# Paired 512-column products and GpSimd weight sums in the fast feed-forward tiles of a two-layer transformer kernel

## The reference, cut to what matters

```
def swiglu(h, w1, w3, w2):
    return (jax.nn.silu(h @ w1) * (h @ w3)) @ w2
...
x = x + 0.5 * rms_norm(swiglu(rms_norm(x, g[0]), ffn_w1[l, 0], ffn_w3[l, 0], ffn_w2[l, 0]), g[1])
...
x = x + 0.5 * rms_norm(swiglu(rms_norm(x, g[4]), ffn_w1[l, 1], ffn_w3[l, 1], ffn_w2[l, 1]), g[5])
```

## Time and profile before

| what | value |
|---|---|
| runs | 1863.45, 1861.57, 1861.51 us; median 1861.57 us |
| profiled execution | 1861.66 us, its span 1859.7 us |
| granted TensorE clock over the span | 1.000 |
| busy | TensorE 99%, weight loads 91%, VectorE 71%, ScalarE 49%, GpSimd 3% |
| chain of waits that ended last | TensorE 85%, VectorE 9%, ScalarE 3% |
| DMA | 174.64 MB, mean 94 GB/s |

### The profile page before, as it was taken

The page is one execution under the profiler, slowest core; times in us unless marked ns, Lnnn a source line. Parts: engine busy times, 40 slices in busy tenths (PEclk is TensorE's granted clock), DMA queues, the critical chain, the costliest instruction groups (busy, mean ns, idle before and its releaser), DMA issues.

```text
span 1859.7 us, 31170 instructions
## 1 busy us (share of the span) xinstructions
PE 1842.6 (99%) x12175; PEld 1693.9 (91%) x12175; DVE 1318.0 (71%) x1742; ACT 914.3 (49%) x1386; POOL 53.6 (3%) x51
## 2 busy tenths in 40 slices
PE   8999999999999999999999999999999999999999
PEld 7899988988889899998898999989988898999888
DVE  6888862487656888882288888822888488888623
ACT  6455552355545545562255555622666464455522
POOL 0000000011100000000000000000000000000000
PEclk9999999999999999999999999999999999999999
DMA  6244343232223333333323343333221232343331
GB/s 183 80 113 113 91 115 102 79 90 72 77 57 102 91 91 106 97 104 106 108 57 108 91 113 104 102 98 104 63 63 57 69 91 84 99 112 105 109 102 47
DMA packets 339464, 174.64 MB, mean 94 GB/s; under 512 B 11070, under 2 KB 337836, under 8 KB 339372
## 3 DMA queue, kind: packets, MB, share of 16 engines
q1 hardware_dynamic: 338656, 172.25, 33.0%
q10 hardware_dynamic: 716, 1.11, 0.2%
HBM read 171.24 MB, written 2.10 MB: 93 GB/s over the span
## 4 chain that ended last, share of the span: by engine, by line
PE 85%; DVE 9%; ACT 3%; issue 2%; DMA 0%; POOL 0%; DVEq 0%; SPq 0%; ACTq 0%
PE acc L1881 19%; PE acc L1882 19%; PE acc L1883 19%; PE duo L1881 9%; PE duo L1883 9%; PE duo L1882 9%; DVE wl L1175 2%; DVE xg L1220 1%; DVE mx L1534 1%; PE acc L2147 1%; DVE probT L1555 1%; ACT prob L889 1%; DVE y L1240 1%; ACT wh L641 0%; DVE xT L1247 0%
## 5 line engine op out<-in xcount | busy, mean ns | idle before, releaser
L1881 PE MATMUL acc<-xg,wh 128*128 128x256 f32 (+1 forms) x1040 | 340.4, 327 | 2.4 <-DVE xg L1220 1.0
L1883 PE MATMUL acc<-xg,wl 128*128 128x256 f32 (+1 forms) x1040 | 336.9, 324 | 0.0
L1882 PE MATMUL acc<-xg,wh 128*128 128x256 f32 (+1 forms) x1040 | 336.8, 324 | 0.0
L1175 DVE TENSOR_TENSOR wl<-raw,wh 128x1024 fp32r<-128x1024 f32 (+2 forms) x198 | 228.9, 1168 | 126.5 <-ACT wh L641 126.2
L1882 PE MATMUL acc<-hT,wh 128*128 128x512 f32 (+1 forms) x704 | 255.2, 363 | 0.0
L1881 PE MATMUL acc<-hT,wh 128*128 128x512 f32 (+1 forms) x704 | 255.2, 363 | 0.0
L1883 PE MATMUL acc<-hT,wl 128*128 128x512 f32 (+1 forms) x704 | 255.2, 362 | 0.0
L641 ACT ACTIVATE wh<-raw 128x1024 fp32r<-128x1024 f32 (+2 forms) x198 | 194.4, 1011 | 116.4 <-PE acc L1883 71.8
L1881 PEld LDWEIGHTS acc<-xg,wh 128*128 128x128 f32 x1040 | 197.7, 190 | 20.5 <-issue 3.1
L1883 PEld LDWEIGHTS acc<-xg,wl 128*128 128x128 f32 x1040 | 197.7, 190 | 15.8
L1882 PEld LDWEIGHTS acc<-xg,wh 128*128 128x128 f32 x1040 | 197.9, 190 | 14.9
(11 more groups left out here) (283 smaller groups left out, 4175.6 us busy)
## 6 DMA issues: line engine op xcount, KB each, us to landing
raw<-in_ffn_w_dram SPq DMA_DIRECT2D x238, 512.0 KB, 4.2
raw<-in_ffn_w_dram SPq DMA_DIRECT2D x32, 384.0 KB, 3.4
raw<-in_moba_w_qkv_dram SPq DMA_DIRECT2D x24, 512.0 KB, 3.8
raw<-in_moba_w_o_dram SPq DMA_DIRECT2D x8, 512.0 KB, 3.8
raw<-in_mla_w_o_dram SPq DMA_DIRECT2D x8, 512.0 KB, 3.7
xin<-in_x_dram SPq DMA_DIRECT2D x4, 512.0 KB, 5.4
raw<-in_mla_w_dq_dram SPq DMA_DIRECT2D x4, 512.0 KB, 3.9
raw<-in_mla_w_uq_dram SPq DMA_DIRECT2D x8, 256.0 KB, 2.9
```

Source lines behind the costliest of these rows:

```text
L1175: v.tensor_tensor(wl[:, slot, 0:tiles], raw[:, slot, 0:tiles], f32(wh[:, slot, 0:tiles]), ALU.subtract).then_inc(w_lo, 1)
L1881: t.matmul(dst, w_h, m_h, start=start, stop=False, skip_group_check=onto)
L1882: t.matmul(dst, w_h, m_l, start=False, stop=False, skip_group_check=onto)
L1883: return t.matmul(dst, w_l, m_h, start=False, stop=stop, skip_group_check=onto)
```

## The change

In the fast tiles:

- `paired` takes the place of `tiles`: for each step of k one matmul with the high weights streams the high and the low part of the moving operand as 512 columns into a pair of 256-column accumulators (one bank), and one with the low weights streams the high part alone, 256 columns, onto the first of the pair. Before, there were three matmuls of 256 columns.
- Every accumulator is now a pair, so P3 gets a bank of its own (`acc[2 + j]`), `usum` is joined by `gsum` (which lies over `cosT` and `sinT`), ScalarE's copies are 512 columns each and one more, and VectorE's `gate_row` and `up_row` each add 128 x 1024 and then `fold` the pairs (128 x 512).
- The weight sums leave VectorE: GpSimd's `weight_sums` makes them with three operations per tile (128 x 512, 128 x 512, 128 x 1024). The second waits until the previous tile's third low part has read `ssum`; SyncE's `read` waits for the third as well.
- The rope tables are loaded in three of the four feed-forward stages, ahead of the down products, in place of the two earlier places.

```diff
-        usum = at("usum", [P, 4, HALF], F32, rb_at)
+        usum = at("usum", [P, 2, 2, HALF], F32, rb_at)
+        gsum = at("gsum", [P, 2, 2, HALF], F32, cos_at)
...
-            return acc[j], duo[j][:].rearrange("p (a s) -> p a s", s=HALF)
+            def pairs(bank):
+                return bank[:].rearrange("p (a l s) -> p a l s", l=2, s=HALF)
+
+            return pairs(acc[j])[:, 0], pairs(duo[j]), pairs(acc[2 + j])[:, 0]
...
-                def read(w):
-                    sp.wait_ge(w_lo, w + 2)
+                def read(f):
+                    sp.wait_ge(w_lo, tile_unit(u0, f) + 2)
+                    sp.wait_ge(ssum_ready, 3 * (FAST * FFN_STAGE[st] + f - FS) + 3)
...
+            def weight_sums(st):
+                g0, u = FAST * FFN_STAGE[st], U0[st] + (len(KV_U) if st == KV_ST else 0)
+                def tile_sums(f, j, counts):
+                    n, w, a, b = 3 * (g0 + f - FS), tile_unit(u, f), raw[:, 2 * j], raw[:, 2 * j + 1]
+                    for i in range(2):
+                        pool.wait_ge(raw_full[2 * j + i], counts[i])
+                    g.tensor_tensor(b[:, 0:KH], b[:, 0:KH], b[:, KH:KD], ALU.add).then_inc(ssum_ready, 1)
+                    pool.wait_ge(ssum_ready, n + 1)
+                    pool.wait_ge(w_lo, w)
+                    g.tensor_tensor(ssum[:, 0:KH], b[:, 0:KH], a[:, 0:KH], ALU.subtract).then_inc(ssum_ready, 1)
+                    pool.wait_ge(ssum_ready, n + 2)
+                    g.tensor_tensor(ssum[:, KH:3 * KH].rearrange("p (a k) n -> p a k n", a=2), raw[:, 2 * j:2 * j + 2, KH:KD],
+                                    ssum[:, 0:KH].unsqueeze(1).broadcast_to([P, 2, KH, P]), ALU.subtract
+                                    ).then_inc(ssum_ready, 1)
+                with pool.Fori(FS // 2, KF // 2) as it:
+                    for j in range(2):
+                        tile_sums(2 * it + j, j, [landed[tile_unit(u, FS + j) + i] + 16 * (it - FS // 2)
+                                                  for i in range(2)])
...
-                    s.activation(usum[:, 0], tile_banks(j)[0][:, half(0)], COPY).then_inc(copied, 1)
+                    s.activation(gsum[:, 0], tile_banks(j)[0], COPY).then_inc(copied, 1)
...
-                    s.activation(usum[:, 2:4], tile_banks(j)[1][:, 2:4], COPY).then_inc(copied, 1)
+                    s.activation(usum[:, 0], tile_banks(j)[2], COPY)
+                    s.activation(usum[:, 1], tile_banks(j)[1][:, 1], COPY).then_inc(copied, 1)
...
+                if table is not None:
+                    s.dma_start(cosT[:], table[0]).then_inc(table_in, 16)
+                    s.dma_start(sinT[:], table[1]).then_inc(table_in, 16)
...
+                def fold(dst, sums):
+                    return v.tensor_tensor(dst[:].rearrange("p (a s) -> p a s", a=2), sums[:, :, 0], sums[:, :, 1], ALU.add)
+
                 def gate_row(f, w, g, banks):
                     dve.wait_ge(unit_done, w + 3)
                     dve.wait_ge(copied, 3 * g + 3)
-                    v.tensor_tensor(T[0][:].rearrange("p (a s) -> p a s", a=2), banks[1][:, 0:4:3], usum[:, 0:2],
-                                    ALU.add).then_inc(rows_ready, 1)
+                    v.tensor_tensor(gsum[:], banks[1], gsum[:], ALU.add).then_inc(rows_ready, 1)
+                    dve.wait_ge(rows_ready, 4 * g + 1)
+                    fold(T[0], gsum).then_inc(rows_ready, 1)
...
-                    outer_sums(w + 4, g + 1, slot, counts)
-                    inner_sums(g + 1, slot)
                     tile_lo(w + 4, 0, slot)
                     tile_lo(w + 4, 1, slot)
                     gate_row(f, w, g, banks)
...
+            def paired(dst, slot, first, moving, start=True):
+                for k in range(KH):
+                    m = moving(k)
+                    w_h, w_l = wh[:, slot, first + k], wl[:, slot, first + k]
+                    t.matmul(dst, w_h, m, start=start and k == 0, stop=False, skip_group_check=True)
+                    ins = t.matmul(dst[:, 0], w_l, m[:, 0], start=False, stop=k == KH - 1, skip_group_check=True)
+                return ins
...
-                    tiles(running, 0, 0, KH, quarter(0, 0)).then_inc(prod_psum, 1)
+                    paired(running, 0, 0, quarter(0, 0)).then_inc(prod_psum, 1)
```

More of the change, by code:

```diff
@@ L511, in ffn @@
                         if i < SLOTS:
-                            read(tile_unit(u0, KF - 2 + i // 2))
+                            read(KF - 2 + i // 2)
                         else:
@@ L611, in _ @@
             rsqrt(RT0[N_PRE2])
+            weight_sums(2)
             post_norm(N_F1)
@@ L722, in x_update, with ffn @@
                 x_squares(t, n_pre, 1)
-            def ffn(st, n_post, g_pre, g_post, kv=None):
+            def ffn(st, n_post, g_pre, g_post, table, kv=None):
                 nth = FFN_STAGE[st]
@@ L968, in _ @@
             split(5)
-            ffn(0, N_F0, gain(0, 0, 0), gain(0, 1, 0))
+            ffn(0, N_F0, gain(0, 0, 0), gain(0, 1, 0), rope_a)
             u, r = U0[1], R0[1]
@@ L1031, in _ @@
             split(U0[2] + 5)
-            ffn(2, N_F1, gain(0, 4, 0), gain(0, 5, 0))
+            ffn(2, N_F1, gain(0, 4, 0), gain(0, 5, 0), rope_r)
             u, r = U0[KV_ST], R0[KV_ST]
@@ L1464, in ffn @@
                     for j in range(2):
-                        fast(2 * it + j, j, hid[:, bass.ds(2 * it + j, 1)].rearrange("p a s -> p (a s)"),
-                             [c + 16 * (it - FS // 2) for c in counts_of(FS + j + 1)])
-                fast(KF - 2, 0, hid[:, KF - 2], counts_of(KF - 1))
+                        fast(2 * it + j, j, hid[:, bass.ds(2 * it + j, 1)].rearrange("p a s -> p (a s)"))
+                fast(KF - 2, 0, hid[:, KF - 2])
                 def hidden_lo(i):
@@ L2023, in quarter @@
                 def quarter(i, j):
-                    return lambda k: (xg[:, 0, KH * i + k, half(j)], xg[:, 1, KH * i + k, half(j)])
+                    return lambda k: xg[:, :, KH * i + k, half(j)]
                 def xsum(i):
-                    return lambda k: (tx[:, i, 0, k], tx[:, i, 1, k])
+                    return lambda k: tx[:, i, :, k]
                 def fast(f, j, first=False):
                     w, g = tile_unit(u, f), FAST * nth + f - FS
-                    running, apart = tile_banks(j)
-                    running = running[:, half(0)]
+                    running, apart, fourth = tile_banks(j)
                     def x_wait(semaphore, count):
@@ L2053, in fast @@
                     pe.wait_ge(copied, 3 * g + 1)
-                    tiles(running, 2, 0, KH, xsum(2), start=False, onto=True).then_inc(prod_psum, 1)
+                    paired(running, 2, 0, xsum(2), False).then_inc(prod_psum, 1)
                     x_wait(xb_lo, 4)
                     pe.wait_ge(copied, 3 * g + 2)
-                    tiles(apart[:, 3], 2, KH, KH, quarter(1, 1), start=False, onto=True).then_inc(unit_done, 1)
+                    paired(apart[:, 1], 2, KH, quarter(1, 1), False).then_inc(unit_done, 1)
                     pe.wait_ge(copied, 3 * g + 3)
-                    tiles(running, 3, 0, KH, xsum(3), start=False, onto=True).then_inc(unit_done, 1)
+                    paired(running, 3, 0, xsum(3), False).then_inc(unit_done, 1)
                 for j in range(2):
```

60 lines of the change are left out of this document (21 added, 39 removed).

## The result

Median 1918.65 us (1917.88 to 1919.50, four runs) against 1861.56 us before: ratio 1.0304 [1.0286 to 1.0322], **slower by 57 us**. The prediction said 1902.5, between 1868 and 1940.

The account below looks back on a forecast made before the run. TensorE bounds the old kernel at 10.08 us a tile; after the change VectorE, alternating with GpSimd, would. +5.6 and +4.6 make +10.2 us a stage, +41 for four: 1861.7 + 41 = 1902.5 us, range 1868 to 1940.

Parts of the forecast that it names:

- rival A: The forecast itself: VectorE and GpSimd exclude each other in fast tiles, 10.49 us a tile, 1888 to 1914 us; chance 0.62.
- Rival B: VectorE and GpSimd pass each other in fast tiles: 9.74 us a tile, 1854.5 us, faster; chance 0.11.
- Rival C: GpSimd's sums in fast tiles cost more, the wide one 3.2 us, or block fully: 1936 to 1949 us; chance 0.17.
- D: GpSimd's sums find better cover beside gate and up sums: rounds of 10.1 to 10.2 us, 1878 to 1885 us; chance 0.07.
- E: Moving operands in two pieces of 256 stream as two products, saving TensorE nothing; 1876 us if the engines pass; chance 0.03.
- A round: VectorE's chain of splits, sums, folds and hand-overs with GpSimd in one fast tile: 10.49 us, where TensorE wants 9.71.
- dependent ones stand 0.04 apart: Step of VectorE's round in the fast tiles: an instruction needing the one before starts 0.04 us after it.
- The first interval: Start of a stage's fast tiles, from tile 6 to VectorE's first rounds; with the later rounds forecast at +5.6 us a stage.
- VectorE begins the first round at T+5.65: Step at a stage's start, T being tile 6's start: third split ends at T+4.55, an x part follows, then the round.
- The end of the stage: VectorE's hidden split in tile 21 comes late: +4.6 us a stage, paid at k = 6 of the first down product.
- TensorE's own gain: Fast tiles: 0.0133 us saved per product, 28 pairs a tile, 9.71 for 10.08 us; 24 us for 64 tiles if TensorE stayed the bound.
- The rest at nothing: Rope table loads, SyncE's loads and norm factors cost nothing; with cover gone, each 1 to 4 us once per stage.

Follow-up runs that it names:

- e1: The kernel before with only the weight sums moved to GpSimd; products, copies and row sums as before: 1866.99 us, ratio 1.0025.
- e3: The changed kernel with GpSimd's three sums per tile replaced by memsets of the same places, so it writes but reads nothing: 1875.11 us, ratio 1.0072.
- e6: The changed kernel with the gate fold as a tensor_reduce, one SBUF operand instead of two: 1908.20 us, ratio 1.0252.
- e2: The changed kernel with the four weight sums back on VectorE, GpSimd idle in the fast tiles: 1964.85 us, ratio 1.0553.
- e5: From e2, low halves of the paired accumulators left unread: 256-column copies, row sums of 512, no fold: 1848.46 us, ratio 0.9925.
- e4: The changed kernel with VectorE's split of hidden rows 6 to 9 moved ahead of the up row in the last fast tile: 1914.55 us, ratio 1.0284.

## Why the prediction was right, and where its terms were off

The **mechanism** held as forecast (rival A): a VectorE instruction with two SBUF operands and a reading GpSimd instruction exclude each other, the third split is late, P5 waits. The prediction says "both read two SBUF operands"; that is narrower than its own rows, since the mask step at 369.22 has one operand in SBUF and takes 2.35 us beside the splits, where the same step takes 0.34 at 1335.4. The links of the chain, as they stand above: first split 1.22 (forecast the same); GpSimd's second sum 1.15 after it; second split 1.07 after that (1.08 forecast); the wide sum 2.28 (2.29); the fold 0.55 (0.55). Undisturbed, e1 has the wide sum at 2.40, for the 2.43 taken from bounds. e3 took away GpSimd's reads, e6 the gate fold's second SBUF operand, and the stretching went with them; e1 and e2 made each half alone, and e2 was 103 us slower than before, e1 5 (1.9 of them the slow start). Rival B (the engines pass each other, 1854.5) falls by the stretched rows of after. Its price was wrong as well: e3, which is what B looks like, came to 1875, with tiles of 9.97 to 10.00 for the 9.74 that B reckoned "by TensorE and the copies". Rival C (1936 and up) falls by the 2.28, D (shorter rounds) by the 10.65, E (pieces of 256 as two products) by e5's 9.71.

The Trainium skill (SBUF — State Buffer, Who interferes with whom) has the later engine blocked for the whole instruction. Its pairing rule (two SBUF inputs of VectorE against a GpSimd instruction that reads SBUF, not one that only writes it) agrees with every run here. But the waiting instruction ends its duration less 0.12 to 0.15 after the other, in all four handovers read, so the full blocking, an estimated 0.56 more a tile, is not there.

The **sum** was 16 us short (+41 for +57), by these terms:

- *A round*, forecast 10.49, measured 10.65. The step that failed is "dependent ones stand 0.04 apart" for the product at L1354: inside the loop it stands 0.23 after the up fold, in all 56 tiles of the loops, and the same gap was there before (L1321). Tile 20, which is written out behind the loop, has 0.03 (fold from 244.11 to 244.80, product at 244.83), so the gap goes with the loop's form; why is not shown. The other steps came 0.03 shorter in all. +0.16 x 13 intervals: +2.0 a stage.
- *The first interval*, forecast about 10.3 with "VectorE begins the first round at T+5.65", measured 11.77. That step left out GpSimd: its second sum is released by the third split, so in the first round it comes in during the x part and holds the first split up:

```profile
85.52 2.22 POOL L621 TENSOR_TENSOR ssum<-raw 128x512 f32<-128x512 f32 x1 [14.65 <-DVE wl L1420]
...
86.50 2.32 DVE L1420 TENSOR_TENSOR wl<-raw,wh 128x1024 fp32r<-128x1024 f32 x1
```

  The 2.32 are 1.22 and 1.1 of waiting. With what is left from the sum's other steps: +1.5 a stage. Together with the rounds that is 9.1 instead of 5.6, 14 us for four.
- *The end of the stage*, forecast +4.6 at k = 6, measured 1.8 + 2.3 = 4.1. I had it all at one place. Part is paid earlier, in tile 21, where ScalarE's own hidden split (247.69 to 249.16) stands ahead of the copies that P6 waits for; the rest stands at k = 6:

```profile
250.18 0.50 PE L1912 MATMUL duo<-xg,wh 128*128 128x512 f32 x1 [1.20 <-ACT usum L840]
...
259.50 0.50 PE L1893 MATMUL acc<-hT,wh 128*128 128x512 f32 x1 [2.13 <-DVE hT L1483]
```

  Two us less than forecast for four stages.
- *Half clock*, not forecast: 3.2 us. In stages two and four the products behind the gap come 0.43 apart, with the granted clock at 0.54 over this stretch, close to its lower level of half (the table by stretch of after, columns as in e5):

```profile
852.50:856.00 3.50, 3.50 (x10) 2.73 (x9) 3.50 (x2) 3.50 (x5) 0.00 (x0) 0.54 0.05 16
```

41 + 14 - 2 + 3 = 56.

**TensorE's own gain** was a step that this kernel hides: 24 us forecast, 13 found in e5. The saving of 0.0133 a pair is right while tiles last 9.71; at 9.89 it is 0.007. It decides nothing here, since VectorE is the bound, but it would have, had VectorE kept up. In after the slower pairs show too: from the start of P1 to that of P4 it is 4.16 in early tiles and 4.24 in later ones.
The Trainium skill (TensorE: Matmul & The Clock Gate, Back-to-back issue gap), by its gap for an isolated product, would give 0.0025 a pair, an estimated tile of 10.01. The measured tile of 9.71, and of 9.89 later, is below that: for this stream of loads and products its gap is too small a price for an instruction.

**The rest at nothing** held for rope tables, loads and norm factors: SyncE's loads are not late in any fast tile, and nothing waits for the norm factors. One cover I had not named: the four splits of `tx` per stage go from 4.62 to 9.02 us beside GpSimd's three sums for the first tile (7.9 in the third stage). Tile 7 of the first stage begins at 91.05 all the same (91.12 before); in the third stage the cover falls short, by 0.6 us here and by 1.5 in e1.

## What to carry to other kernels

Joining two product streams of the busiest engine into one saved it only 0.0133 us per product dropped, at best, and each joined accumulator must be taken apart again by an engine that may be full: price the taking apart first, since here the row sums take VectorE 2.5 us more a tile (3.8 by the starts in e2, 1.3 in e1) against 0.37 saved on TensorE. Work given to GpSimd is not wholly taken off VectorE as long as GpSimd reads SBUF and VectorE reads two SBUF operands. One operand in PSUM or a reduction on VectorE's side, or a memset on GpSimd's, let them run together here, and some exclusion costs nothing where the waiting engine has slack (e1). Walk the first and the last tile of a loop through the new chain as well as the middle: here two fifths of a stage's loss lie at those edges (1.1 + 1.8 + 2.3 of 13.1).

## What the runs showed of the hardware that I had not expected

- Two engines that exclude each other take turns, instruction by instruction, even where one has its work back to back. The four `tx` splits of after, beside GpSimd:

```profile
62.93 9.02 DVE L1410 TENSOR_TENSOR tx<-tsum,tx 128x1024 fp32r<-128x1024 f32 x4
...
63.09 2.22 POOL L621 TENSOR_TENSOR ssum<-raw 128x512 f32<-128x512 f32 x1 [3.00 <-DVE wl L1208]
65.39 3.26 POOL L623 TENSOR_TENSOR ssum<-raw,ssum 128x1024 f32<-128x1024 f32 x1
68.60 2.27 POOL L618 TENSOR_TENSOR raw<-raw 128x512 f32<-128x512 f32 x1
```

  The four took 4.62 before; the three sums take 1.29, 2.40 and 1.29 alone. Together that is 9.6 us of work, and both engines are done with it after 9.0: in such a stretch two engines are worth little more than one.
- Pairs of 512- and 256-column products stream 2% slower after some tiles (0.3467 to 0.353), at a granted clock of 1.00 in both stretches (e5). The single 256-column products of before and of e1 stay at 10.08 a tile in every stage. The cause is open.
- The first product after a wait is followed by the next after 0.33 instead of 0.235 (after: 162.46 to 162.79): a restart costs 0.1 us beside the wait.
- Stretches at half clock (granted 0.54) stand at TensorE's long waits in the down product: starts 2.5 to 3.1 us apart at k = 6 in all four stages of after, e2, e3 and e6, with half clock in two, one, three and two of them; starts 2.0 apart in e4, with none; none in before and e5, which have no such wait. The one other stretch inside a kernel (e6, last stage) stands behind a wait of P5 with starts 2.45 apart. So each stretch goes with a wait, but only about half of the waits bring one; what decides it no run here shows.
